# Strassen's seven products for most chunks of the two up projections of a decoder layer

## The reference

```python
def swiglu(x, wi, wo):
    gate, up = jnp.split(x @ wi, 2, axis=-1)
    return (jax.nn.silu(gate) * up) @ wo

hp = layer_norm(ALPHA * x + 0.5 * swiglu(x, wi1, wo1))      # first half
qa, ka, va, qb, kb, vb, qi, ki, wi = project(hp, w_in, ...) # then two attention mixers
h = layer_norm(ALPHA * h + concat(o_a, o_b) @ w_out)
h = layer_norm(ALPHA * h + 0.5 * swiglu(h, wi2, wo2))       # second half
y = h + (p @ ple_proj) * jax.nn.sigmoid(h @ ple_gate)
```

## Time and profile before

| | us |
|---|---|
| three runs | 1452.3, 1453.84, 1459.82 (median 1453.84) |
| profiled execution | 1451.17 |
| its span, first to last instruction | 1449.5 |
| mean granted TensorE clock | 0.981 of full |

### The profile page before, as it was taken

The page is one execution under the profiler, slowest core; times in us unless marked ns, Lnnn a source line. Parts: engine busy times, 40 slices in busy tenths (PEclk is TensorE's granted clock), DMA queues, the critical chain, the costliest instruction groups (busy, mean ns, idle before and its releaser), DMA issues.

```text
span 1449.5 us, 30740 instructions
## 1 busy us (share of the span) xinstructions
PE 1366.3 (94%) x12059; PEld 1263.4 (87%) x12059; DVE 543.5 (37%) x1340; ACT 455.1 (31%) x841; POOL 638.0 (44%) x455
## 2 busy tenths in 40 slices
PE   7999999999989999999885796989999999999988
PEld 7899999999979879975663565979999999999888
DVE  3222222200252246788899323272222222200454
ACT  3222222211262343257653421162222222211541
POOL 3344444455465645222465504644433334453642
PEclk9999999999999999999997998999999999999999
DMA  6399665766355533432396897444656567665121
GB/s 248 112 264 321 241 204 197 265 230 206 119 182 177 158 84 103 138 113 59 100 334 207 280 320 275 149 135 149 213 189 215 187 220 256 221 223 172 59 74 44
DMA packets 88960, 269.84 MB, mean 186 GB/s; under 512 B 28210, under 2 KB 28595, under 8 KB 88601
## 3 DMA queue, kind: packets, MB, share of 16 engines
q1 hardware_dynamic: 81160, 253.24, 51.9%
q0 software_dynamic: 6656, 12.60, 3.2%
q10 hardware_dynamic: 1040, 2.62, 1.2%
HBM read 259.78 MB, written 109.10 MB: 254 GB/s over the span
## 4 chain that ended last, share of the span: by engine, by line
PE 82%; DVE 9%; POOL 3%; issue 2%; ACT 2%; DMA 2%; ACTq 0%; SPq 0%; DVEq 0%; POOLq 0%
PE bank L1614 22%; PE bank L1618 22%; PE bank L1616 22%; DVE idx_scores L1456 2%; DVE idx_scores_left L1402 2%; POOL w_rest L579 2%; DVE topk_lists L1401 2%; PE bank L1662 2%; PE bank L2158 1%; PE bank L1664 1%; PE bank L1663 1%; DMA cache_a_ring<-in_cache_a 1%; PE bank L1974 1%; PE bank L1986 1%; PE bank L1964 1%
## 5 line engine op out<-in xcount | busy, mean ns | idle before, releaser
L579 POOL TENSOR_TENSOR w_rest<-w_raw,w_high 128x1024 fp32r<-128x1024 f32 (+2 forms) x159 | 410.2, 2580 | 602.6 <-ACT w_high L747 601.6
L747 ACT ACTIVATE w_high<-w_raw 128x1024 fp32r<-128x1024 f32 (+2 forms) x159 | 180.1, 1133 | 767.6 <-PE bank L1618 733.5
L1614 PE MATMUL bank<-x_high,w_high 128*128 128x272 f32 x1808 | 377.5, 290 | 8.7 <-DVE x_rest L1024 8.7
L1618 PE MATMUL bank<-x_high,w_rest 128*128 128x272 f32 x1808 | 375.1, 289 | 0.0
L1616 PE MATMUL bank<-x_rest,w_high 128*128 128x272 f32 x1808 | 373.8, 288 | 0.0
L1614 PEld LDWEIGHTS bank<-x_high,w_high 128*128 128x128 f32 x1808 | 284.9, 189 | 15.5 <-POOL w_rest L579 8.6
L1616 PEld LDWEIGHTS bank<-x_rest,w_high 128*128 128x128 f32 x1808 | 285.1, 189 | 0.0
L1618 PEld LDWEIGHTS bank<-x_high,w_rest 128*128 128x128 f32 x1808 | 283.3, 190 | 0.0
L1056 DVE SCALAR_TENSOR_TENSOR hidden<-silu_gate,bank 128x272 f32<-128x272 f32 x88 | 34.6, 434 | 386.8 <-ACT silu_gate L767 386.8
L1614 PE MATMUL bank<-hidden_high,w_high 128*128 128x272 f32 x616 | 127.7, 288 | 0.0
L1618 PE MATMUL bank<-hidden_high,w_rest 128*128 128x272 f32 x616 | 127.5, 288 | 0.0
(11 more groups left out here) (317 smaller groups left out, 1829.5 us busy)
## 6 DMA issues: line engine op xcount, KB each, us to landing
out_a_sample<-in_cache_a SPq DMA_DIRECT2D x73, 1344.0 KB
w_raw<-in_w_wi SPq DMA_DIRECT2D x88, 512.0 KB, 5.1
cache_a_ring<-in_cache_a SPq DMA_DIRECT2D x112, 384.0 KB, 5.8
w_raw<-in_w_wo SPq DMA_DIRECT2D x32, 704.0 KB, 5.6
w_raw<-in_w_w_in SPq DMA_DIRECT2D x26, 512.0 KB, 3.7
kv_b_pages<-in_cache_b POOLq DMA_DIRECT2D x96, 64.0 KB, 4.9
w_raw<-in_w_gate SPq DMA_DIRECT2D x8, 640.0 KB, 3.9
bias_toeplitz<-rev_bias POOLq DMA_DIRECT2D x32, 128.0 KB, 2.6
```

Of the source, the lines that this page charges most:

```text
L579: nc.gpsimd.tensor_tensor(rest_part(u0, i, j)[:, 0:tiles, :], RAW[:, slot, 0:tiles, :], high_part(u0, i, j)[:, 0:tiles, :].bitcast(F32), A ...
L747: nc.scalar.activation(high_part(u0, i, j)[:, 0:tiles, :], RAW[:, slot, 0:tiles, :], ACT.Copy).then_inc(S["hi_ready"], 1)
L1614: mm(banks[n][:, 0:HALF], wh, xh[n], start=start, stop=False)
L1618: last = mm(banks[n][:, 0:HALF], wl, xh[n], start=False, stop=stop)
```

## The change

In chunks 4 to 19 of the first up stage and 2 to 19 of the second, 34 of 44, gate and up product are made as one 2 x 2 block product by Strassen's scheme in Winograd's form. The weights of a chunk are a block matrix: A11, A12 the gate rows for features 0 to 511 and 512 to 1023 (4 tiles each), A21, A22 the up rows. The blocks of x are B11, B12 (features 0 to 511, first and second token half), B21, B22. Seven products of 4 tiles and 272 tokens replace eight:

| product | weights | x |
|---|---|---|
| 0 | A11 | B11 |
| 1 | A21 + A22 - A11 | x_two = B22 - (B12 - B11) |
| 2 | A21 + A22 | x_one = B12 - B11 |
| 3 | A11 - A21 | x_three = B22 - B12 |
| 4 | A12 | B21 |
| 5 | A12 - (A21 + A22 - A11) | B22 |
| 6 | A22 | x_four = B21 - x_two |

- Once per stage VectorE makes the four sums of x (`token_sums`), ScalarE their highs (`x_highs`), VectorE their rests. They stand ahead of the stage's first hidden and silu.
- Per chunk VectorE makes four sums of 512 columns of weights out of `w_raw` (`weight_sums`, and a fourth in `seven`) and the rest of product 3's weights; ScalarE makes seven highs of 512 columns (`op_high`); GpSimd the other six rests (`op_rest`). Their place is a ring of four operand slots in what was `w_high` and `w_rest`, so a slot is split again when the product four before is done.
- Product 0 is copied out by ScalarE (`first_plus_sixth`), then four banks serve: 4 is added to 0, 5 to 2 and 6 to 3 in PSUM, and VectorE makes five sums with a bank, hidden's product over 544 columns with both inputs in SBUF, and hidden's rest. Hidden's high moves to ScalarE.
- The loops now have four chunks in their body. Tables move to other addresses, some semaphores are merged, and the load of `p_raw` waits for chunk 19 of the second stage.

The parts of the diff on which the following rests, in this order: GpSimd's rests, ScalarE's chunk, VectorE's sums of weights and the first half of its chunk, TensorE's chunk:

```diff
+            def op_rest(w, i, d, o):
+                wait_high(pool, w, i, d, o)
+                high, low = op_parts(w, i, d, o)
+                nc.gpsimd.tensor_tensor(low, w_operand(w, i, d, o), high.bitcast(F32), ALU.subtract
+                                        ).then_inc(S["lo_ready"] if o >= 5 else S["op_rest"], 1)
...
+                for o in (4, 5, 6):
+                    op_rest(w, i, d, o)
+                if not is_last(w, i, d):
+                    for o in (0, 1, 2):
+                        op_rest(w, i, d + 1, o)
...
+                def seven(i, d, only=False):
+                    wait_product(act, which, i, d, 0)
+                    act.wait_ge(S["h_done"], chunk_at(which, i, d) + (KF * which - 1))
+                    nc.scalar.activation(VS[:, s, :], banks[0][:, 0:HALF], ACT.Copy).then_inc(S["first_sb"], 1)
+                    op_high(i, d, 4)
+                    wait_product(act, which, i, d, 3 if which == 1 and last else 1)
+                    op_high(i, d, 5)
+                    if d > 0:
+                        hidden_high(i, d - 1)
+                    wait_product(act, which, i, d, 4 if which == 1 and last else 2)
+                    op_high(i, d, 6)
+                    if not last:
+                        wait_product(act, which, i, d, 3)
+                        op_high(i, d + 1, 0)
...
+                    wait_product(act, which, i, d, 4)
+                    nc.scalar.activation(SG[:, s, 0:HALF], banks[0][:, 0:HALF], ACT.Silu)
+                    if not last:
+                        op_high(i, d + 1, 1)
+                        wait_product(act, which, i, d, 5)
+                        op_high(i, d + 1, 2)
+                    wait_part(act, which, i, d, "c12")
+                    nc.scalar.activation(SG[:, s, HALF:T], SG[:, s, HALF:T], ACT.Silu).then_inc(S["silu_done"], 1)
+                    if not last:
+                        wait_product(act, which, i, d, 6)
+                        op_high(i, d + 1, 3)
...
+                def weight_sums(i, d):
+                    a11, a21, a22 = RAW[:, gate, 0:4, :], RAW[:, up, 0:4, :], RAW[:, up, 4:8, :]
+                    v.tensor_tensor(E3[:], a11, a21, ALU.subtract).then_inc(S["sum_ready"], 1)
+                    v.tensor_tensor(a21, a21, a22, ALU.add).then_inc(S["sum_ready"], 1)
+                    if not (isinstance(i, int) and i == 0 and d == 0):
+                        dve.wait_ge(S["lo_ready"], i * 8 + (u0 + 2 * (SEVEN_FROM[which] + d) - 1))
+                    dve.wait_ge(S["sum_ready"], seven_at(which, i, d, 4, 2))
+                    v.tensor_tensor(E2[:], a21, a11, ALU.subtract).then_inc(S["sum_ready"], 1)
...
+                def seven(i, d):
+                    wait_high(dve, which, i, d, 3)
+                    v.tensor_tensor(low, E3[:], high.bitcast(F32), ALU.subtract).then_inc(S["op_rest_d"], 1)
+                    dve.wait_ge(S["op_rest"], seven_at(which, i, d, 4, 2))
+                    v.tensor_tensor(E2[:], RAW[:, raw_of(which, i, d, 0)[0], 4:8, :], E2[:], ALU.subtract
+                                    ).then_inc(S["sum_ready"], 1)
+                    dve.wait_ge(S["first_sb"], seven_at(which, i, d, 1, 1))
+                    wait_product(dve, which, i, d, 1)
+                    v.tensor_tensor(vs, vs, banks[1][:, 0:HALF], ALU.add).then_inc(S["part_done"], 1)
+                    if d > 0:
+                        hidden_rest(i, d - 1)
...
+                def seven(i, d):
+                    pe.wait_ge(S["h_done"], c + (KF * which - 1))
+                    for o in range(7):
...
+                        out = BANK[4 * s + (0, 1, 2, 3, 0, 2, 3)[o]][:, 0:HALF]
+                        for k in range(4):
+                            xh, xl = x_operand(o, k)
+                            mm(out, high[:, k, :], xh, start=o < 4 and k == 0, stop=False, skip_group_check=True)
+                            mm(out, high[:, k, :], xl, start=False, stop=False, skip_group_check=True)
+                            last = mm(out, low[:, k, :], xh, start=False, stop=k == 3, skip_group_check=True)
```

More of the change, by code:

```diff
@@ L768, in pair, with x_highs @@
                         last.then_inc(S["silu_done"], 1)
-                pair(0, lambda i, j: None if which == 1 and j == 2 else high(u0, i, j, 8))
+                def x_highs():
+                    if which == 1:
+                        act.wait_ge(*rest_done(1, 1, REST_ON_POOL[-1]))
+                    act.wait_ge(S["t_part"], 8 * which + 4)
+                    for t in (1, 0, 2, 3):
+                        src, out = TS[t], TH[t]
+                        if t == 3:
+                            out = out.rearrange("p (a b) n -> p a b n", b=2)
+                        nc.scalar.activation(out, src, ACT.Copy).then_inc(S["t_high"], 1)
@@ new lines, in silu @@
+                def silu(i, s):
+                    if not (isinstance(i, int) and i == 0 and which == 0):
+                        act.wait_ge(S["h_done"], 22 * which + i * 2 + s - 1)
+                    act.wait_ge(S["unit_used"], u0 + i * 4 + 2 * s + 1)
+                    for n in range(2):
+                        last = nc.scalar.activation(half(SG, s, n), BANK[4 * s + n][:, 0:HALF], ACT.Silu)
+                    last.then_inc(S["silu_done"], 1)
+                before = SEVEN_FROM[which] // 2 - 1
@@ L771, in up_stage @@
+                for i in range(before + 1):
+                    for j in (2, 3):
+                        if not (which == 1 and i == 0 and j == 2):
+                            high(u0, i, j, 8)
+                    if i == 0:
+                        x_highs()
+                    silu(i, 0)
+                    if i < before:
+                        for j in (4, 5):
+                            high(u0, i, j, 8)
+                        silu(i, 1)
                 if which == 0:
-                    pair(1, lambda i, j: high(u0, i, j, 8))
@@ L773, in up_stage @@
                     act.wait_ge(S["rev_in"], 1)
                     nc.scalar.dma_start(REV_DRAM, spread(REV[:], 1, REV_COPIES)).then_inc(S["rev_out"], 16)
-                with act.Fori(2 - which, UP_ITERS - 1) as i:
-                    pair(i, lambda i, j: high(u0, i, j, 8))
+                act.wait_ge(S["unit_used"], u0 + 4 * before + 3)
+                for o in (0, 1):
+                    op_high(0, 0, o)
+                silu(before, 1)
+                act.wait_ge(S["unit_used"], u0 + 4 * before + 4)
@@ L777, in up_stage @@
+                for o in (2, 3):
+                    op_high(0, 0, o)
+                with act.Fori(0, SEVEN_LOOPS[which]) as i:
+                    for d in range(4):
+                        seven(i, d)
+                if which == 0:
+                    act.wait_ge(S["rev_out"], 16)
+                for d in range(SEVEN_TAIL[which]):
+                    seven(SEVEN_LOOPS[which], d)
                 pair(UP_ITERS - 1, lambda i, j: high_of(u0 + 4 * i + j))
@@ L1066, in up_stage, with hidden @@
-                if which == 0:
-                    hidden(0)
-                    keep_tables()
-                with dve.Fori(1 - which, UP_ITERS) as i:
-                    hidden(i)
+                def hidden(i, s):
+                    done = i * 2 + (22 * which + s + 1)
+                    c = i * 2 + s
+                    dve.wait_ge(S["silu_done"], done)
+                    dve.wait_ge(S["unit_used"], u0 + i * 4 + 2 * s + 2)
+                    for n in range(2):
+                        last = v.scalar_tensor_tensor(half(HF, s, n), half(SG, s, n), 0.5,
+                                                      BANK[4 * s + 2 + n][:, 0:HALF], ALU.mult, ALU.mult)
+                    last.then_inc(S["h_done"], 1)
+                    dve.wait_ge(S["h_done"], done)
+                    v.tensor_copy(HH[:, bass.ds(c, 1), :], HF[:, s:s + 1, :]).then_inc(S["hh_done"], 1)
+                    dve.wait_ge(S["hh_done"], done)
+                    v.tensor_tensor(HL[:, bass.ds(c, 1), :], HF[:, s:s + 1, :],
+                                    HH[:, bass.ds(c, 1), :].bitcast(F32), ALU.subtract
+                                    ).then_inc(S["hl_done"], 1)
@@ new lines, in up_stage @@
+                before = SEVEN_FROM[which] // 2 - 1
+                for i in range(before + 1):
+                    hidden(i, 0)
+                    if i < before:
+                        hidden(i, 1)
+                        keep_tables()
+                weight_sums(0, 0)
+                hidden(before, 1)
+                with dve.Fori(0, SEVEN_LOOPS[which]) as i:
+                    for d in range(4):
+                        seven(i, d)
+                if which == 0:
+                    dve.wait_ge(S["rev_out"], 16)
@@ L1655, in up_stage @@
                     pair(1, tables=True)
-                with pe.Fori(2 - which, UP_ITERS) as i:
-                    pair(i)
+                pe.wait_ge(S["t_part"], 8 * which + 8)
+                with pe.Fori(0, SEVEN_LOOPS[which]) as i:
```

(5 more changed lines are left out.)

241 lines of the change are left out of this document (206 added, 35 removed).

## The result

The changed kernel takes 1492.4 us (median of 4 runs, 1486.0 to 1495.8), the kernel before 1453.2 (1452.3 to 1459.8): a ratio of 1.026, 95% interval 1.023 to 1.029, slower. The profiled execution has a span of 1493.0 us against 1449.5.

What follows compares the result with a forecast made beforehand. TensorE's matmul count bounded the up stages; after the change, VectorE and GpSimd excluding each other would. Profiled execution 1451.2 + 30 (chunks) + 10.5 (starts) = 1491.7, so 1492 us, range 1470 to 1512.

Steps and rivals of the forecast that it cites:

- The mechanism: In seven-product chunks, two-SBUF-input VectorE operations and GpSimd operations exclude each other by whole instructions: 10.83 us a chunk in sequence.
- the CAST in the earlier trace: VectorE copy at 127.78, ending 0.30 us after a GpSimd operation; read as a one-input operation that also waits for GpSimd.
- The chunk: Each of 34 seven-product chunks: 12.90 us in place of 12.03, +0.87 us each, +30 us in all.
- Both hand-overs through ScalarE: Twice a chunk, a ScalarE split between VectorE's sum and GpSimd's rest: 0.08, 0.63 and 0.08 us before GpSimd's start.
- 0.78 - 0.64: GpSimd's start before it asks for SBUF, put at 0.13 us, leaving each of six rests holding for 1.17 us.
- The starts: One-time delays where x sums and copies precede the first hidden and silu: 4.4 us in stage 1, 6 in stage 2.
- The idle time itself: TensorE idle at the starts: 4.4 us in stage 1, 2.3 and 3.8 us in stage 2.
- the clock: TensorE's granted clock in the up stages: waits might lower it below nine tenths, but counted at nothing.
- Loads: Weight loads in the up stages: enough slack after the slot is free, so 0 us; bound +15 us.
- A: Rival: VectorE and GpSimd do not collide in the seven-product chunks; 1411 us, chance 0.12.
- B: Rival: they collide but queue so gaps are mostly filled, chunk 10.83 to 11.7 us; 1440 us, chance 0.13.
- C: Rival: weight-load waits come on top, or register waits cost more, 0.5 us a chunk and 15 once; 1524 us, chance 0.10.

Runs made afterwards that it cites:

- experiment 1: Changed kernel with seven VectorE operations per chunk taking their second input from a PSUM bank, not SBUF (results not the reference's): 1425.1 us, ratio 0.980.
- experiment 2: Changed kernel with each GpSimd rest issued as two instructions of half the size: 1470.8 us, ratio 1.014.
- experiment 8: Changed kernel with two rests moved to VectorE, reordered starts, later cache copies, hidden's high ahead of operand 5's inside every next chunk: 1421.0 us, repeated 1422.0.
- experiment 6: Changed kernel with two rests moved to VectorE and reordered starts, plus product 3's weight sum issued ahead of hidden's rest: 1461.8 us, ratio 1.009.
- experiment 11: Changed kernel with only hidden's high put ahead of operand 5's on ScalarE, high and rest inside every next chunk: 1470.2 us, ratio 1.012.
- experiment 9: Kernel of experiment 8 with the rest of operand 0 made ahead of the weight sums instead of behind them: 1432.9 us, ratio 0.988.
- experiment 4: Changed kernel with only the starts reordered: sums of x before table copies in stage 1, first silu before copies of x in stage 2: 1483.5 us, ratio 1.021.

## Why the prediction was right

**The mechanism** was right, and experiments 1 and 2 show it: for these operations the meeting needs VectorE's second input in SBUF, and it lasts for one whole instruction. That a copy with one input also waits, which the prediction took from the CAST in the earlier trace rows, no experiment tests. The Trainium skill (GPSIMD Engine Reference, section 1, Specifications) names two SBUF inputs as a case of contention; here it was 1.78 against 0.68 us.

**The chunk**, forecast 12.90 us, is 12.73. Both hand-overs through ScalarE take 0.75 us from the end of the sum to GpSimd's start, not 0.79, which is 0.08 of the 0.17; the cause of the rest is open. (0.78 - 0.64 is 0.14, not 0.13; that moves the forecast chunk by under 0.1 us.) 34 chunks cost 34 x 0.70 = 24 us in place of 30: mis-sized by 6 us (by the mean of 12.69 it is 22 us, and 2 us more fall to what comes once). TensorE's waits stand ahead of the second product, as forecast, and on a bank sum.

**The starts** were mis-sized the other way: 10.5 us forecast, 10.2 + 2.0 + 3.3 = 15.5 measured (3.3 is what stage 2's 15.9 us are above 18 chunks at 0.70). The idle time itself was right (4.46 us against 4.4 in stage 1, 1.79 and 3.06 against 2.3 and 3.8 in stage 2); the term that was wrong is the clock, which I counted as nothing because slices of 36 us at half load showed nines. Windows of 4 us show what such a slice hides, and the kernel before had it already: there TensorE is idle for 2.37 and 1.56 us at 964 to 967, and its clock is at 0.50 in the window in which that ends. The middle's 2.6 us I had not forecast either. Its 1.5 us in the last layer norm stand in a window at 0.57, where the same place in the kernel before had 1.00. TensorE had been idle for 1.94 us ahead of both, so why the clock fell in one of them is open, as is the cause of the other 1.1 us. First the kernel before, then the changed one:

```profile
957.00:961.00 4.00, 3.91 (x89) 2.65 (x89) 1.99 (x7) 2.41 (x5) 2.99 (x3) 1.00 0.31 77
...
965.00:969.00 4.00, 2.44 (x9) 1.97 (x8) 4.00 (x8) 2.04 (x5) 3.08 (x3) 0.50 0.71 250
```

```profile
980.00:984.00 4.00, 3.91 (x61) 2.87 (x62) 1.51 (x5) 2.43 (x5) 2.50 (x3) 0.57 0.27 62
```

**Loads**: 0 us forecast, one wait of 4.18 us shown. It cost TensorE about 1.8 us: it is idle for 2.82 us ahead of that chunk's second product in place of 0.99. Beyond it the slack was read rightly for a chunk of 12.7 us. It is used up at a faster chunk (17 us of waits in stage 1 in experiment 8).

24 + 15.5 + 2.6 and 0.7 us more in the chunks of stage 1 make 43 us, the difference of the spans (43.5), where the prediction had 40.5. That the time came out on the number is luck: two errors of 5 to 6 us had opposite signs, and the runs of the changed kernel alone lie 10 us apart.

**The rivals.** A (no collision, 1411 us) is what experiment 1 makes by other data: 1425 us, with the starts as they were. So the collision is worth 67 us, not the 81 between the forecast and A. B (gaps filled by a better order) is not reached by order alone: 12.1 us against its 11.4. C's waits came where an experiment asked earlier (31 us in experiment 6) or made the chunk shorter (17 us in experiment 8).

## What to carry to other kernels

Two engines with room in their busy time are not two resources if their instructions exclude each other: add up what both hold, and if that is above the pace of the bound, move an operation to the one that would be waiting. Moving two operations of a chunk was worth 45 us here. Order counts too (22 us in experiment 11, 12 us the other way in experiment 9), but judge it by the time and not by one meeting: which of two operations came first changed between two executions of the same program. And put an operation whose input comes by DMA behind those that TensorE waits for in its engine's queue.

## What the hardware showed beside

- Splitting GpSimd's instruction (1.29 us into two of 0.73) shortened VectorE's longest meetings by 0.56 us and the kernel by 22 us, though it adds six instructions a chunk.
- Behind 4.46 us without a matmul TensorE's granted clock was 0.50 for 4 us, and 0.50 once more 12 us later. Behind idle stretches of 1.5, 1.7 and 2.2 us within 8 us (experiment 4, start of stage 2) it was 0.50 in 1017 to 1019 us, 0.80 and 0.77 as means of the 4 us windows around; behind one of 1.3 us (up to 30.44 us there) it stayed at 1.00.
- A busy share can mislead in a window: experiment 9 has TensorE busy for 50.00 of 50 us with 377 matmuls, experiment 8 with 402. Count instructions.
